# Expert blocks of 32 rows in four column quarters, with a second buffer for gathered rows

## What is computed

```
grp = argmax(x @ router_g_w + b)                      # one of 4 groups
top_v, top_i = top_k(e_logits of that group, 2)       # two of its 8 experts
gates = p_grp * softmax(top_v)
hdn = silu(xb @ wg[e]) * (xb @ wu[e])                 # 1024 -> 512, for the rows of expert e
y[token] += (hdn @ wd[e]) * gate                      # 512 -> 1024
x = x + gate2 * y ; out = rmsnorm(x)
```

## Time and profile before

| | us |
|---|---|
| median of 3 runs (lowest, highest) | 3250.87 (3242.91, 3257.13) |
| the profiled execution | 3251.47 |
| its span | 3249.6 |
| TensorE busy in it | 2959.1 |
| VectorE, ScalarE, GpSimd busy | 1411.0, 973.6, 161.1 |

### The profile page before, as it was taken

How to read it: one execution, slowest core, us unless ns; L and a number is a source line. 1 busy time by engine, 2 the same in 40 slices (tenths; PEclk the granted TensorE clock), 3 DMA queues, 4 the chain that set the end, 5 groups by cost and what they waited for, 6 DMA issues and landing times. The chain is left out here.

```text
span 3249.6 us, 68199 instructions
## 1 busy us (share of the span) xinstructions
PE 2959.1 (91%) x28667; PEld 1753.5 (54%) x28668; DVE 1411.0 (43%) x3438; ACT 973.6 (30%) x1872; POOL 161.1 (5%) x248
## 2 busy tenths in 40 slices
PE   5998999999999388988988599959999999999988
PEld 2432455454545378888877255535555555555543
DVE  2245466665556446666656144451222221122217
ACT  2456343433334223333332112102222222222215
POOL 0000000000000000000000000000000000000004
PEclk8999999999999799999998799969999999999998
DMA  7631123242322685566641743455786478667658
GB/s 271 210 124 55 49 98 115 101 148 89 109 101 85 198 214 152 152 169 170 183 137 36 235 148 116 141 158 203 287 314 255 153 269 300 256 231 275 254 195 329
DMA packets 373370, 575.74 MB, mean 177 GB/s; under 512 B 31246, under 2 KB 231110, under 8 KB 370088
## 3 DMA queue, kind: packets, MB, share of 16 engines
q1 hardware_dynamic: 335112, 470.72, 42.9%
q0 software_dynamic: 18080, 72.10, 6.3%
q10 hardware_dynamic: 19968, 29.83, 3.1%
HBM read 427.04 MB, written 145.54 MB: 176 GB/s over the span
## 5 line engine op out<-in xcount | busy, mean ns | idle before, releaser
L451 PE MATMUL pj_P<-pj_hT,pj_wc 128*128 128x448 f32 (+2 forms) x1600 | 590.4, 516 | 0.9 <-ACT pj_stage L579 0.9
L2491 PE MATMUL moe_PG<-wgu,moe_xT 128*64 128x256 f32 x5248 | 582.4, 380 | 0.7 <-ACT moe_xT L2389 0.7
L2491 PEld LDWEIGHTS moe_PG<-wgu,moe_xT 128*64 128x64 f32 x5248 | 378.1, 137 | 226.8 <-issue 50.5
L451 PEld LDWEIGHTS pj_P<-pj_hT,pj_wc 128*128 128x128 f32 x1600 | 294.1, 189 | 256.5 <-issue 239.4
L2498 PE MATMUL moe_PTY<-wd,moe_hT 128*64 128x512 f32 x1312 | 317.7, 603 | 0.0
L2392 ACT ACT_TABLE_LOAD x82 | 105.2, 1283 | 483.0 <-issue 482.9
L1978 PE MATMUL merge_PO<-merge_w,merge_mT 128*128 128x512 f32 x544 | 241.8, 603 | 1.7 <-DMA merge_w<-in_w_out 1.7
L1978 PEld LDWEIGHTS merge_PO<-merge_w,merge_mT 128*128 128x128 f32 x544 | 103.8, 194 | 126.7 <-issue 124.6
L2355 DVE COPY moe_hT<-moe_PH 128x128 f32<-128x128 f32 x164 | 47.9, 292 | 282.9 <-PE moe_PH L2483 282.0
L2351 DVE TENSOR_TENSOR moe_sg<-moe_sg,moe_PG 128x128 f32<-128x128 f32 x164 | 46.4, 283 | 282.5 <-ACT moe_sg L2392 282.5
L2358 DVE COPY moe_y<-moe_PTY 128x512 f32<-128x512 f32 x82 | 56.7, 692 | 208.3 <-PE moe_PTY L2498 208.3
(11 more groups left out here) (385 smaller groups left out, 4208.2 us busy)
## 6 DMA issues: line engine op xcount, KB each, us to landing
wgu<-in_w_gate SPq DMA_DIRECT2D x32, 2048.0 KB, 9.4
wgu<-in_w_up SPq DMA_DIRECT2D x32, 2048.0 KB, 14.9
wd<-in_w_down SPq DMA_DIRECT2D x32, 2048.0 KB, 16.6
re_hkf<-scratch_hk SPq DMA_DIRECT2D x60, 640.0 KB, 8.0
re_rkf<-scratch_rk SPq DMA_DIRECT2D x68, 320.0 KB, 6.8
scratch_hk<-pj_hk SPq DMA_DIRECT2D x16, 1344.0 KB
scratch_y_rows<-moe_y ACTq DMA_DIRECT2D x164, 128.0 KB, 5.1
scratch_rk<-pj_rk SPq DMA_DIRECT2D x16, 1120.0 KB, 4.4
```

Source lines behind the costliest of these rows:

```text
L451: ins = eng.matmul(bank[:, 0:wp], wc[:, j, k, :], hT[:, k, k0:k0 + wp], start=(k == 0), stop=(k == KD - 1), skip_group_check=True)
L2491: ins = eng.matmul(PG[64 * c:64 * c + 64, j, 0:256].rearrange("p (a b) -> p a b", a=2), x_rows, wgu[p][:, :, k, o:o + 128], start=(k == 0) ...
```

## The change

BLOCK becomes 32, with at least 2 blocks per expert; there are now up to 200 blocks, 202 row blocks in `y_rows` and a zero block in front. A row is gathered in quarters of 256, onto partitions 32 q + p. `xg` is 128 x 256, and POOL copies it to a second buffer `xc`, which TensorE turns. `gate_up` has four matmuls side by side in each of its 8 steps, `down` four in each of 4 steps, of 256 columns each. `down` of a block comes after `gate_up` of the next, and its y is copied and stored one block later, in four stores of 32 KB. One sigmoid per block remains, and the table is asked for ahead of the loop. The tiles' sums are made by two scans. The mask of tokens moves from `is_block` to `is_place`.

```diff
-BLOCK = 64
-MAX_BLOCKS = T * TOP_K // BLOCK + N_EXPERTS
+BLOCK = 32
+MIN_BLOCKS = 2
+MAX_BLOCKS = T * TOP_K // BLOCK + MIN_BLOCKS * N_EXPERTS
...
# SP
-                        eng.wait_ge(ev("y_made"), done)
+                        eng.wait_ge(ev("y_made"), done + 1)
...
# DVE
-                for n in range(NT):
...
-                    step(eng.tensor_tensor(carry[:, n + 1, :], carry[:, n, :], src, ALU.add))
+                for h, experts_of in enumerate((slice(0, CUT), slice(CUT, N_EXPERTS))):
+                    n = NT * (experts_of.stop - experts_of.start)
+                    step(eng.tensor_tensor_scan(carry[:, experts_of, :].rearrange("p e n -> p (e n)"), restart[:, experts_of, :].rearrange("p e n -> p (e n)"),
+                                                PTY[:, h, 0:n], 0.0, ALU.mult, ALU.add))
...
+                def keep_y(g):
+                    eng.wait_ge(ev("y_made"), g)
+                    eng.wait_ge(ev("y_out"), g * 64)
                     eng.tensor_copy(y[:, :], PY[:, :]).then_inc(ev("y_kept"), 1)
+                with eng.Fori(0, n_blocks) as g:
+                    eng.wait_ge(ev("sigmoid_made"), g + 1)
+                    eng.tensor_tensor(sg[:, :], sg[:, :], PG[:, 0, 0:128], ALU.mult).then_inc(ev("silu_made"), 1)
+                    eng.wait_ge(ev("silu_made"), g + 1)
+                    eng.tensor_tensor(hid[:, :], sg[:, :], PG[:, 0, 128:256], ALU.mult).then_inc(ev("hid_ready"), 1)
+                    eng.wait_ge(ev("h_turned"), g + 1)
+                    eng.tensor_copy(hT[:, :], PH[:, 0, 0:128]).then_inc(ev("hT_kept"), 1)
+                    keep_y(g + 1)
+                keep_y(n_blocks + 1)
...
# ACT
+                eng.preload_act_table_set("sigmoid_and_others")
...
+                def store_y(g):
+                    for n in range(4):
+                        eng.dma_start(t["y_rows"][ds(g * BLOCK, BLOCK), 256 * n:256 * n + 256], y[32 * n:32 * n + 32, :]).then_inc(ev("y_out"), 16)
+                    eng.sem_inc(ev("row_blocks"), 16)
-                with eng.Fori(total(eng), MAX_BLOCKS + 1) as g:
+                with eng.Fori(n_blocks + 1, MAX_BLOCKS + 2) as g:
                     eng.dma_start(t["y_rows"][ds(g * BLOCK, BLOCK), :], zeros[:, :]).then_inc(ev("row_blocks"), 16)
...
+                with eng.Fori(0, n_blocks) as g:
                     eng.wait_ge(ev("gu_made"), g + 1)
+                    eng.activation(sg[:, :], PG[:, 0, 0:128], ACT.Sigmoid).then_inc(ev("sigmoid_made"), 1)
                     eng.wait_ge(ev("x_turned"), g + 1 + 2)
                     eng.copy(xT[:, :, :], PT[:, :, :]).then_inc(ev("xT_kept"), 1)
                     eng.wait_ge(ev("y_kept"), g + 1 + 1)
+                    store_y(g)
...
# POOL
+                with eng.Fori(1, n_blocks + 1) as g:
+                    eng.wait_ge(ev("gathered"), g * 16)
                     eng.tensor_copy(row[:, 0:1], rows[:, ds(g, 1)]).then_inc(ev("row_ready"), 1)
+                    eng.wait_ge(ev("x_turned"), g)
+                    eng.sem_inc(ev("move_begun"), 1)
+                    eng.tensor_copy(xc[:, :], xg[:, :]).then_inc(ev("x_moved"), 1)
                     eng.wait_ge(ev("row_ready"), g + 1)
+                    eng.wait_ge(ev("x_moved"), g)
+                    gather()
...
# TensorE
+                def gate_up(g, p):
+                    eng.wait_ge(ev("xT_kept"), g + 1)
                     for k in range(KD):
+                        x_rows = xT[:, k % 2, 32 * (k // 2):32 * (k // 2) + 32]
+                        for q in range(4):
+                            ins = eng.matmul(PG[32 * q:32 * q + 32, 0, 0:256].rearrange("p (a b) -> p a b", a=2), x_rows, wgu[p][:, :, k, 128 * q:128 * q + 128],
                                              start=(k == 0), stop=(k == KD - 1))
...
+                def down(g, p):
+                    eng.wait_ge(ev("hT_kept"), g)
+                    eng.wait_ge(ev("y_kept"), g + 1)
+                    for k in range(KE):
+                        for n in range(4):
+                            ins = eng.matmul(PY[32 * n:32 * n + 32, :], hT[:, 32 * k:32 * k + 32], wd[p][:, k, 256 * n:256 * n + 256],
+                                             start=(k == 0), stop=(k == KE - 1))
+                def rest_of_expert(g0, count, p):
+                    with eng.Fori(1, count) as b:
+                        g = g0 + b
+                        gate_up(g, p)
+                        turn(g + 1)
+                        down(g, p)
+                        turn_hid(g)
```

More of the change, by code:

```diff
@@ L2264, in _ @@
                 eng.wait_ge(ev("x1_in"), 16 * N_KEPT)
-                eng.wait_ge(ev("y_made"), total(eng))
+                eng.wait_ge(ev("y_made"), total(eng) + 1)
                 for n in range(N_KEPT, NT):
@@ L2342, in _ @@
+                step(eng.tensor_scalar(quarter[:, :], quarter[:, :], -1.0, 3.0, ALU.mult, ALU.add))
+                step(eng.memset(PY, 0.0))
                 eng.wait_ge(ev("rows_made"), 1)
-                step(eng.tensor_scalar(rows[:, :], PH[:, 0, 0:MAX_BLOCKS + 1], 2.0, second_half[:, :], ALU.mult, ALU.add))
+                step(eng.tensor_scalar(rows[:, :], PH[:, 0, 0:MAX_BLOCKS + 1], 4.0, quarter[:, :], ALU.mult, ALU.add))
                 eng.sem_inc(ev("rows_ready"), 1)
[L2346 to L2357, removed]
-                    eng.tensor_copy(y[:, :], PY[:, :]).then_inc(ev("y_kept"), 1)
@@ L2492, in gate_up @@
                                              start=(k == 0), stop=(k == KD - 1))
-                    ins.then_inc(ev("g_made" if j == 0 else "gu_made"), 1)
-                def down(p, j, c):
-                    for n in range(2):
-                        ins = eng.matmul(PY[64 * n:64 * n + 64, :], hT[:, j, 64 * c:64 * c + 64], wd[p][:, 2 * c + j, 512 * n:512 * n + 512],
-                                         start=(j == 0 and c == 0), stop=(j == 1 and c == 1))
-                    return ins
@@ L2502, in _ @@
-                turn(0)
-                with eng.Fori(0, N_EXPERTS // 2) as i:
-                    before, first, second = blocks_of_pair(eng, i)
-                    for p in range(2):
-                        eng.wait_ge(loaded[p][0], i * 16 + 16)
-                        eng.wait_ge(loaded[p][1], i * 16 + 16)
-                        eng.sem_inc(ev("expert_begun"), 1)
-                        with eng.Fori(0, (first, second)[p]) as b:
-                            g = before + b if p == 0 else before + first + b
-                            eng.wait_ge(ev("xT_kept"), g + 1)
-                            gate_up(p, 0)
-                            gate_up(p, 1)
-                            turn_hid(g, 0)
-                            turn(g + 1)
-                            eng.wait_ge(loaded[p][2], i * 16 + 16)
-                            eng.wait_ge(ev("hT_kept"), g * 2 + 1)
-                            eng.wait_ge(ev("y_kept"), g + 1)
-                            down(p, 0, 0)
-                            turn_hid(g, 1)
-                            down(p, 0, 1)
-                            eng.wait_ge(ev("hT_kept"), g * 2 + 2)
-                            down(p, 1, 0)
-                            down(p, 1, 1).then_inc(ev("y_made"), 1)
-                            eng.nop()
@@ new lines, in rest_of_expert, with next_expert @@
+                def rest_of_expert(g0, count, p):
[5 more added lines that the diff above has]
+                        turn_hid(g)
+                        eng.nop()
+                def next_expert(g, i, p):
+                    for matrix in range(2):
+                        eng.wait_ge(loaded[p][matrix], i * 16 + 16)
+                    eng.sem_inc(ev("expert_begun"), 1)
+                    gate_up(g, p)
+                    turn(g + 1)
+                    down(g, 1 - p)
+                    turn_hid(g)
+                    eng.wait_ge(loaded[p][2], i * 16 + 16)
+                    eng.sem_inc(ev("down_begun"), 1)
@@ new lines, in _ @@
+                turn(0)
+                before, first, second = blocks_of_pair(eng, 0)
+                for matrix in range(3):
+                    eng.wait_ge(loaded[0][matrix], 16)
+                eng.wait_ge(ev("xT_kept"), 1)
+                gate_up(before, 0)
+                turn(before + 1)
+                turn_hid(before)
+                rest_of_expert(before, first, 0)
+                next_expert(before + first, 0, 1)
+                rest_of_expert(before + first, second, 1)
+                with eng.Fori(1, N_EXPERTS // 2) as i:
+                    before, first, second = blocks_of_pair(eng, i)
+                    next_expert(before, i, 0)
+                    rest_of_expert(before, first, 0)
+                    next_expert(before + first, i, 1)
+                    rest_of_expert(before + first, second, 1)
@@ L2528, in _ @@
+                n_blocks = total(eng)
+                down(n_blocks, 1)
                 eng.wait_ge(ev("all_stored"), 1)
```

122 lines of the change are left out of this document (65 added, 57 removed).

## The result

| | before | after |
|---|---|---|
| median (lowest, highest), us | 3249.66 (3242.91, 3257.13), 8 runs | 3259.36 (3255.59, 3266.57), 8 runs |
| span of the profiled execution | 3249.6 | 3257.7 |
| the expert loop in it | 959.6 | 960.7 |
| blocks | 82 | 150 |

The changed kernel is slower by 0.3%: ratio 1.0032, 95% interval 1.0018 to 1.0046. The forecast was 3290, with 3215 to 3330 as its range; the measured change is 9.7 us where 39 were forecast.

A forecast was written before the change was run, and what follows sets the result against it. TensorE alone was taken to bound the expert loop, 959.6 us, with transfers hidden. A loop of 908 plus 78 of stall gives 986, 26 more; with 13 at the start, 3251.5 + 26 + 13 = 3290 us, range 3215 to 3330.

The forecast's parts named there:

- both chains: Expert loop's transfer loops, gathers and y stores: 7.8 and 7.2 us under weights, both over the block's 6.02.
- The fixed lag: Expert loop's transfers under weight loads: the landing's addition is fixed, not by size, so smaller stores save little.
- rival 1: Expert loop: transfers don't bind, the addition under weights going by packets; loop 908, total 3213, faster; chance 0.20.
- the stall: Expert loop: time lost to gathers and y stores under weight loads, 2.6 us per expert, 30 times, 78 us.
- The gather chain: POOL's loop of gather, landing, row copy, move to xc, next gather: 7.8 us under weights, 4.8 light.
- the y chain: DVE's copy of y, ACT's four stores, last landing, next copy: 7.2 us under weights, 4.6 light.
- The late y round: Expert loop, y rows under weights: a landing of 4.8 plus 2.4, so 7.2 us.
- The floor: Expert loop if nothing but TensorE binds: 150 x 6.02 = 903, with its ends 908 us, 52 under 959.6.
- The start: Before the expert loop: ACT's 51 zero stores at 0.87 take 44.4 us, making the first xT copy 13.4 late.
- 2: Expert loop, in between: landings of 5.5 and 4.3, half the 78, total 3251, no change; chance 0.19.
- 3: TensorE in the expert loop: four quarters don't overlap fully; block 7.26, loop 1094, total 3399, slower; chance 0.04.
- 4: POOL's move takes 0.9 and the zero stores 61 us: total 3368; one alone 3307 or 3351; chance with halves 0.13.

The follow-up runs named there:

- the run with two gathers under way: Two buffers for gathered rows ahead of xc, added to the changed kernel with two y buffers and zero stores on SP's queue: 3218.81 us, ratio 0.9897.
- blocks in pairs: Changed kernel with each expert's count rounded up to 64 rows, still in blocks of 32, so 164 blocks: 3328.07 us, ratio 1.0256.

## Why the prediction was wrong

**Right.** The block count, that both chains bind under weights and neither does without, that four quarters at once cost what a pair did (3.66 for the 64 records of `gate_up` against 3.59 worked out, 1.93 for `down` against 1.87), and the lag of the landings. By what the Trainium skill, TensorE: Matmul & The Clock Gate (Part 3, measured speedup), gives, 2.38 for three column tiles, the block would be about 7.4, an estimate from that figure. The trace has 6.085, so the measurement decides against it for four quarters of 32 columns with 256 columns of float32 each.

**The fixed lag** that I put against rival 1 held. A gather of 128 KB takes 2.8 light and 6.05 in the mean of the 71 that take over 5; one of 256 KB took 3.3 and 6.2 to 7.0. Half the bytes save half a microsecond and the lag of some 3 stays. Forecast: 3.0 and 6.0.

**The step that failed is the stall: "So not twice: 30 x 2.6 = 78 us. Loop 908 + 78 = 986."** The mechanism was the right one, the term was mis-sized: it measured 35.5 for the two chains together. The gather chain alone, as the run with two y buffers has it, cost 16, where the prediction had 2.6 per expert, 78, for each of the two. For the y chain two inputs were off, both to one side, and one held:
- The slack in front of `turn_hid`. I counted the 1.2 us between `hid` and `turn_hid` and took ACT to be busy until its sigmoid. Its four issues took 1.76 from the first to the end of the last, and not 2.3 as forecast from those of 64 partitions; they end at 2606.60 in the undisturbed block, and where it is late the sigmoid follows their end by 0.4 (2745.60, 2745.99), so ACT is free at 2607.0, 0.7 before it is needed. Slack 1.85.
- The number of blocks that meet a load. I took 23 us per expert, 30 times, 88 gathers in all (23/7.8 each); 71 of 150 take over 5 us, 2.4 per expert. The time from the gate's issue to the landing of `down`, 20.3 at 2607.83 to 2628.1, is as taken, but not every transfer issued in it is late.
- The late y round held: where DVE waits over 1.5 us for a store it takes 7.4 in the mean of 41 (0.42 the copy, 0.17, 1.43 to the start of the last issue, 5.3 from there to DVE's next copy), where 7.2 was forecast.

With these, 2.4 x (7.4 - 6.085) = 3.2 less 1.85 is 1.3 per expert, an estimate of 39 us for 30 experts; the runs give 35.5 for both chains. This estimate hangs on its inputs: a late round shorter by 0.1 takes 7 us off it. Two things are in the 35.5 that are in no chain: the 1.2 at the one pair of experts above, and 1.7 of a low clock right behind it (last section). For the gather loop the measured round is 6.05 + 0.15 + 0.14 + 0.40 + 0.80 = 7.5 against my 7.8, under 71 gathers and not 88.

**The floor** of 908 was too low by 17, which hid part of the error above: the measured loop without the two chains is 149 x 6.085 + 9.8 + 8.8 (from the last `gate_up` to the end of the last `down`) = 925.2, which is also the loop of the run with two gathers under way. Of the 17, 10 are the 0.065 by which a period is longer than 6.02, and 7 the loss once per pair of experts, which I had not looked for.

**The start**: "51 x 0.87 = 44.4" was 37.9. The term stood on the cadence of stores from 64 partitions; from 32 they follow each other in 0.74, so 13 became 7.5. The bytes' rate did not bind: 51 x 128 KB in 37.9 us is 176 GB/s, where the 19 larger ones went at 219. What does set the 0.74 was not tried.

**Rivals.** 1 (3213, no stall) is wrong as a whole; 2 (3251, "half the 78") came nearest, by its size and not by its landings of 5.5 and 4.3, which are 6.05 and 5.3. 3 is out by the period of 6.085. 4 is out: POOL's move takes 401 ns and the zeros 38 us.

The sum with the measured terms: 3251.5 + (925.2 + 35.5 - 959.6 = 1.1) + 7.5 - 0.5 = 3259.6, where the profiled execution took 3259.8. It closes because the 35.5 are themselves the loop less the 925.2; what it shows is that nothing outside these terms moved. That the total came within 31 of the forecast although the stall was 43 too large is in part luck: the floor was 17 too small, and the two errors have opposite signs. Against the forecast: 43 less stall, 17 more floor, 6 less start.

## What to carry to other kernels

When a stage gets faster than a transfer loop next to it, write the loop as a round (issue, landing, wake, copy, issue) and compare it with the new period, but charge only what exceeds the lead, and take the lead from all the engines on the way, their idle time ahead of the first step too. Two chains of nearly the same round hide each other: freeing one uncovers the other, and only both together gave 35 us here (the gather chain was never freed alone). A second buffer that puts two transfers under way costs a few lines. For the gathers it took away all that was left; for y, shortening the round by three issues did as much (21.7 lost against 26.1).

## What the runs showed that I had not expected

- The lag of a small transfer behind bulk loads: about 3 us for gathers of 256 and 128 KB alike (3.3 to 6.2 or more; 2.8 to 6.05), and about as much for stores of 32 KB (5.3 to the next copy of DVE when late; in the light case one had landed within 2.3). With two gathers and two y buffers it costs nothing.
- A period per pair of experts in which TensorE starts `gate_up` 0.55 us late in every variant, also with no loads and no stalls: by the count of blocks at the boundary of its outer loop, where it reads a word of the table. Before the change the same place cost 0.14. Which of its instructions takes the time was not tried.
- Once, TensorE's clock. After the worst stretch above, with 0.42 and 1.72 us idle, the granted clock falls (columns: us, PE busy, clock, DMA share, GB/s):

```profile
2740.00:2747.00 7.00, 6.58 (x112) 1.00 1.00 360
2747.00:2749.00 2.00, 0.29 (x1) 1.00 0.87 268
2749.00:2751.00 2.00, 1.99 (x24) 0.58 0.98 347
2751.00:2754.00 3.00, 3.00 (x48) 0.71 1.04 394
2754.00:2758.00 4.00, 4.00 (x67) 1.00 1.05 389
```

0.58 is near the lower of its two levels (1.2 of 2.4 GHz). `gate_up` takes 5.35 instead of 3.66 there. It does not follow from the idle time alone: in the kernel with the zero stores on SP's queue the same block has 1.01 and 1.71 us idle ahead of it, the granted clock stays at 1.00, and `gate_up` takes its usual time:

```profile
2747.11 3.66 PE L2533 MATMUL moe_PG<-wgu,moe_xT 128*32 128x256 f32 x64 [1.71 <-issue]
```

In the changed kernel it is the only block after the first with a low clock. The kernel with one row buffer, which waits most, has four slower ones (3.87 to 4.28 us), the one with blocks in pairs has one (5.35), and the other variants have none. So the waits cost their own length and hardly anything more.
